# Constant-table products on TensorE in the second mixer phase of a two-block model

## The reference, cut to what matters

```
# mLSTM, per head h and direction, s = source token, t = target token
dw  = exp(dlog - mt)                       # weights by the gates
s   = (q @ k.T) * dw
num = s @ v ;  den = sum(s)
h   = num / max(|den|, exp(-mt))
# differential attention, per head
a   = softmax(q1 @ k1.T / 8) - lam * softmax(q2 @ k2.T / 8)
y   = rmsnorm(a @ v) * g
```

## Time and profile before

| | us |
|---|---|
| median of 3 runs | 4387.51 |
| lowest and highest | 4380.73 to 4388.9 |
| the profiled execution, its own time | 4394.96 |
| span of its trace, first to last instruction | 4392.9 |
| granted TensorE clock, mean over the span | 0.948 of full speed |
| second mixer phase of layer 0 in that trace | 164.9 |
| second mixer phase of layer 1 in that trace | about 100 |

### The profile page before, as it was taken

The page is one execution under the profiler, slowest core; times in us unless marked ns, Lnnn a source line. Parts: engine busy times, 40 slices in busy tenths (PEclk is TensorE's granted clock), DMA queues, the critical chain, the costliest instruction groups (busy, mean ns, idle before and its releaser), DMA issues. The chain is left out here.

```text
span 4392.9 us, 71554 instructions
## 1 busy us (share of the span) xinstructions
PE 4038.2 (92%) x25458; PEld 3554.2 (81%) x25458; DVE 2368.0 (54%) x4150; ACT 1653.4 (38%) x2543; POOL 1542.2 (35%) x605
## 2 busy tenths in 40 slices
PE   7997798978878999999989999999878799999998
PEld 7974388967656999988879999888766699998887
DVE  4012423134552946687548566785555385667855
ACT  3532203232323443333545433334433254333344
POOL 5740006424003986500018866000051188660000
PEclk9997899989779999999999999999988899999999
DMA  5565544522003554444645544445421255444454
GB/s 186 173 216 190 193 134 148 168 84 72 24 5 103 166 163 140 137 144 144 193 146 164 169 138 141 141 146 182 154 88 41 68 164 169 143 138 140 143 182 153
DMA packets 168398, 614.27 MB, mean 140 GB/s; under 512 B 18592, under 2 KB 20000, under 8 KB 167968
## 3 DMA queue, kind: packets, MB, share of 16 engines
q1 hardware_dynamic: 168224, 611.88, 44.7%
HBM read 610.76 MB, written 1.05 MB: 139 GB/s over the span
## 5 line engine op out<-in xcount | busy, mean ns | idle before, releaser
L1729 POOL TENSOR_TENSOR ring_r<-ring,ring_hi 128x1024 fp32r<-128x1024 f32 x408 | 1070.3, 2630 | 1195.2 <-ACT ring_hi L1866 1194.2
L1866 ACT ACTIVATE ring_hi<-ring 128x1024 fp32r<-128x1024 f32 x792 | 837.9, 1059 | 808.7 <-DMA ring<-in_peer_v 485.6
L1744 PE MATMUL bank<-H_r,ring_hi 128*128 128x256 f32 x3264 | 938.6, 288 | 65.4 <-POOL ring_r L1729 64.3
L1745 PE MATMUL bank<-H_r,ring_hi 128*128 128x256 f32 x3264 | 926.0, 284 | 0.0
L1746 PE MATMUL bank<-H_r,ring_r 128*128 128x256 f32 x3264 | 925.4, 284 | 0.0
L280 POOL TENSOR_TENSOR ring_r<-ring,ring_hi 128x1024 fp32r<-128x1024 f32 x183 | 465.2, 2545 | 642.2 <-ACT ring_hi L274 642.2
L1744 PEld LDWEIGHTS bank<-H_r,ring_hi 128*128 128x128 f32 x3264 | 628.0, 192 | 73.4 <-POOL ring_r L1729 45.3
L1745 PEld LDWEIGHTS bank<-H_r,ring_hi 128*128 128x128 f32 x3264 | 628.4, 193 | 0.0
L1746 PEld LDWEIGHTS bank<-H_r,ring_r 128*128 128x128 f32 x3264 | 628.0, 192 | 0.0
L1796 PE MATMUL bank<-ring_hi,H_r 128*128 128x512 f32 x1536 | 483.6, 396 | 5.2 <-DVE ring_r L2040 5.0
L1798 PE MATMUL bank<-ring_r,H_r 128*128 128x512 f32 x1536 | 475.2, 391 | 0.0
(11 more groups left out here) (309 smaller groups left out, 5562.6 us busy)
## 6 DMA issues: line engine op xcount, KB each, us to landing
ring<-in_peer_u SPq DMA_DIRECT2D x384, 512.0 KB, 3.6
ring<-in_peer_v SPq DMA_DIRECT2D x384, 512.0 KB, 3.6
ring<-in_w_in SPq DMA_DIRECT2D x135, 512.0 KB, 3.7
ring<-in_ada SPq DMA_DIRECT2D x96, 512.0 KB, 5.0
ring<-in_w_f SPq DMA_DIRECT2D x72, 512.0 KB, 4.2
ring<-in_w_br SPq DMA_DIRECT2D x24, 512.0 KB, 3.6
ring<-in_w_q SPq DMA_DIRECT2D x24, 512.0 KB, 3.6
ring<-in_w_out SPq DMA_DIRECT2D x16, 512.0 KB, 3.6
```

The source lines that it names most:

```text
L1729: pool.tensor_tensor(ring_lo[:, slot, :], ring[:, slot, :], ring_hi[:, m % NH, :].bitcast(F32), ALU.subtract).then_inc(p_lo, 1)
L1744: pe.matmul(o, hi[:, k], x_hi_[:, kt, :], start=(kt == 0), stop=False)
L1745: pe.matmul(o, hi[:, k], x_lo_[:, kt, :], start=False, stop=False)
L1866: act.activation(ring_hi[:, m % NH, :], ring[:, (n0 + m) % NS, :], ACT.Copy).then_inc(a_hi, 1)
```

## The change

A helper `fill(o)` issues two fp32 products of the identity matrix with the constant table `iota` (128 by 128) into a place `o` of PSUM. Nobody reads what they write: the real product that follows starts its bank afresh (`start=True`). Both operands lie in SBUF in the tile `CS` from the start of the kernel. The calls are:

```
 def products(h, st):
     if h or st >= 2:
         pe.wait_ge(v_w, 8 * h + 2 * st - 2)
+    fill(bank[1 + st % 2][:, t0:t0 + P])
     pe.matmul(bank[1 + st % 2][:, t0:], mk..., mq...)
...
+def fill(o):
+    for _ in range(2):
+        pe.matmul(o, ident, cc("iota"), start=True, stop=True)
...
 def turn_weights(n):
-    pe.wait_ge(v_p, n + 1)
     if n:
         pe.wait_ge(a_pt, n)
+    for k in range(2):
+        fill(bank[6][:, k * P:(k + 1) * P])
+    pe.wait_ge(v_p, n + 1)
...
 def attend(n):
     h = items[n][0]
-    pe.wait_ge(a_pt, n + 1)
     if n:
         pe.wait_ge(v_o, n)
...
+    fill(bank[7][:, 0:P])
+    pe.wait_ge(a_pt, n + 1)
```

## The result

| | before | after |
|---|---|---|
| median of the runs on one chip, us | 4388.9 (5 runs, 4380.73 to 4400.31) | 4419.93 (5 runs, 4417.44 to 4426.26) |
| the profiled execution, us | 4394.96 | 4423.56 |
| span of its trace, us | 4392.9 | 4421.5 |
| phase of layer 0, us at mean granted clock | 163.3 at 0.71 | 182.1 at 0.83 |
| phase of layer 1, us at mean granted clock | 100.2 at 0.74 | 117.9 at 0.78 |

The ratio of the times is 1.0071, with a 95% interval from 1.0052 to 1.009: 31 us slower, 23 to 40. The forecast was 4415, 27 us slower.

What follows compares the result with a forecast made beforehand. TensorE, busy 92% of the span, stood partly at half clock in the two phases, behind idle waits. Fills on the path 45.1 us less 17.8 from the clock: +27.3, 4415 on the median; range 4392 to 4434 for 8 in 10.

Steps and rivals of the forecast that it cites:

- The places of the fills: Both phases: of 104 fills, 34 hide in waits and 70 lie on the path, 42 in layer 0, 28 in layer 1.
- full clock's price: Both phases: 70 fills on the path at 0.45 us each, 31.5 us; by the clock seen at each place, 45 us.
- the two ends at which the prediction called itself wrong: Mean clock of the phases rising from 0.71 and 0.75 to above 0.9, or staying at 0.71 and 0.75.
- (a): Layer 0, quarter 0 of head 1: fills close the gaps between matmuls, clock 0.69 to 1.00, 3.2 us back.
- (b): Layer 0, quarter 0 of head 0, all at half rate: clock rises before its end, 1.7 us back.
- (c): Layer 0, quarter 3 of heads 1 to 3 and the last head's end: a third of 11.3 us back, 3.8.
- (d): Layer 0, quarter 2: denser matmuls bring the clock back earlier, 0.7 us a head, 2.8 us in all.
- (e): Layer 1, quarters 2 and 3: a third of the 19 us that full clock throughout would give, 6.3 us back.
- Rival 1: Both phases: fills cost and the clock gives nothing back, +45 us, 4433; chance 0.18.
- Rival 2: Both phases: clock holds at 2.4 GHz through the idle stretches, 31.5 us cost, 45.5 back, -14 us, 4373.5; chance 0.08.
- Rival 3: Both phases: about half comes back and the path is shorter than counted, +5 us, 4392.5; chance 0.14.
- A page against the row: Layer 0: clock 0.59 in the quarter after 3.39 us idle, 1.00 after 5.78 us without idle; waits throttle the engine.

Runs made afterwards that it cites:

- gap products: Kernel before, without the change's fills, plus single table products ahead of the long waits before `products` of quarter 2 and `values`: 4348.11 us, ratio 0.9922.
- the waits alone: Kernel before with only the order of the two waits in `turn_weights` and `attend` changed, no fills: 4392.81 us, ratio 1.0013.
- fills as well: The changed kernel with all its fills, plus the gap products ahead of the two long waits: 4390.57 us, ratio 1.0001 to the kernel before.
- half the dose: The gap products kernel with half of its products before each wait (8 instead of 16): 4372.46 us, ratio 0.9960 to the kernel before.
- too many gap products: The gap products kernel with 24 instead of 16 before `products` of quarter 2 (layer 1: 16 instead of 10), heads 1 to 3: 4365.26 us, ratio 0.9950.

## Why the prediction was right, and where it was not

**The places of the fills: right.** The three fills of quarter 1 in layer 0 hide, those in quarters 0 and 3 add themselves, and the fill of `products` stands behind its wait and leaves the longest stretches open (12.2 us before, 15.7 after). That was the core of the forecast, and the gap products, the same table product on the other side of the same wait, show it by reversing the sign. That moving the waits alone costs nothing was taken for granted and holds. One place was wrong: the last `attend` of layer 1 was booked as hidden, and its fill stands behind the wait for ACT's root.

**The price of a fill: wrong for `products`.** The step was "A fill is two of them: 0.45 us at full, 0.85 at half", read from the earlier trace rows, where a 128-row product follows a 128-row product. `products` uses 64 rows (the earlier trace rows says `64*128`), and a fill ahead of it measured 0.74 us. In quarter 2, up to DVE's maxima, it measured 0.64. By these two, 16 fills at 0.74 and 16 at 0.64, an estimate, the fills of `products` cost 7.7 us more than booked, of the 10.8 between the measured 42.3 and the booked 31.5. The rest is a balance: the copy and the overrun above (0.9 us in each of two heads), four fills in head 0's quarter 0, which cost 4.3 us at 0.56, and the end of layer 1, 3.4 us longer, where the last `attend` ran at half rate; against them two quarters 3 that ran at 0.77 without the fills and at 1.00 with them.

**What the clock gives back: the sum about right, its terms not.** At full clock's price the forecast said 31.5 less 4.2 makes 27.3. Measured, 42.3 less 5.8 makes 36.5. The clock rose to 0.83 and 0.78, between the two ends at which the prediction called itself wrong. The two layers came out less well than their sum: 18.8 us for 16 and 17.7 for 12. Term by term, with the fills at their booked prices and one trace on each side:

- (a) Quarter 0 of head 1 came back to 10.77 us at 1.00, as forecast. It can't be put down to the fills alone: it did so without them as well. In layer 0, quarter 0 of heads 1 to 3 ran at 1.00 in 15 of 15 in the kernels with fills in it, and in 15 of 21 in those without. That leaves an effect of the fills open. By this the term is worth about 1 us a head, not 3.2 in one.
- (b) Quarter 0 of head 0 went from 8.57 us at 0.50 to 11.66 at 0.56: some 0.3 us back of the four fills' 3.4 at half rate, not 1.7. The other six kernels without fills took 7.4 to 8.6 us there, and against most of them nothing came back.
- (c) Quarter 3 gave little in heads 1 and 2: 0.53 became 0.58, 0.62 became 0.61, and the quarters grew by 1.36 and 2.37 us. The wait before `values` had not been closed. Behind `values(3, 0)` it gave more than its 3.8: from there to the end of the phase it took 12.78 us at 0.73 before and 10.86 at 1.00 after, with four fills more, one of them hidden, the others booked at 2.6 us. Part of that can be chance, since the waits alone had 11.22.
- (d) Quarter 2 of layer 0 did better than forecast in heads 0 to 2 (0.60 to 0.81, 0.64 to 0.76, 0.59 to 0.76) and no better in head 3 (0.58 to 0.60).
- (e) Layer 1, quarters 2 and 3, gave nothing in head 2, the one of the earlier trace rows: 0.59 before, 0.58 after, 3.5 us longer. In heads 0 and 1 they grew by 2.1 us each (0.68 to 0.73, 0.59 to 0.65), and from `products(3, 2)` to the end by 1.1 (0.62 to 0.73). Against four fills at half rate a head, 3.4 us, and five at the end, that is some 5.7 us back, an estimate, near the 6.3 booked, though spread otherwise.

The rest of the rise lies in quarter 1, 0.77 to 0.96 in head 1. There ACT sets the length, so a higher clock is worth little: the quarter grew by 1.1 us, about one fill of `products` at a low clock. A mean clock over a phase is no account of time.

**Hidden fills.** "In layer 1 it is 0.35 us too long [...] so I book 0": at full clock that is right (quarter 1 of head 1 took 8.05 us with gap products and 8.58 with fills as well, which is less than its fill of `products`), at 0.69 the quarter grew by 3.2 us. A cover read at full clock is too small where the clock can be half.

**The rivals.** Rival 1, a clock that gives nothing back, would have cost 45 us at booked prices and more at the true ones; the phases grew by 36.5, at 0.83 and 0.78. Rival 2 is refuted for this change: with the stretches left open the clock did not hold. That the open stretches are the place where the clock is to be had is what the gap products confirm. Its whole return was put at 45.5 us, and the gap products returned 39.5. With fills as well it would have come out 14 us faster by its price of 31.5; at the true 42.3 it comes out at the time of the kernel before. Rival 3 is refuted too: the interval of the change, 23 to 40 us, begins well above its 5.

The prediction says of *A page against the row* that after 5.78 us without idle time the clock was 1.00. It was 1.00 in them; in the quarter behind them, again without idle time, it was 0.69. So idle time ahead is not all that lowers the clock, and what else does stays open.

So the range held the time although the fills of `products` were booked some 8 us too cheap: the phases grew by 36.5 us where 27.3 were forecast, and the medians differ by 31. That the medians came within 5 us of the forecast is partly luck. The scatter of the start-up, 8 us between the two profiled executions, is large enough for the difference between 36.5 and 31; that it is the cause is not shown.

## What to carry to other kernels

Products that only keep TensorE busy must stand ahead of the wait, in a place of PSUM that nobody waits for; behind the wait they are paid in full, and the stretch stays open. Count the stretch and the products in microseconds at full clock, fill most of it and leave a little: half the dose gave half the gain, though it was enough for quarter 2, and half as many again before `products` lost about half of it. When other work is put ahead of such products, count again, since they then reach past the end of the wait. And price an added matmul by the rows of the array that it and its neighbour use, not by its columns alone.

## What the runs showed of the hardware

- A matmul on 64 rows behind one on all 128 starts 0.64 us after a fill's start, behind one on the same 64 rows 0.44 us: the weight load is exposed in the first case and runs beside the fill in the second. That made 0.74 or 0.45 us of one fill in quarter 0. The load is exposed in the other direction too: the fill's own, behind a product on 64 rows, starts with its first matmul (both at 1207.76 after the change).
- With too many gap products TensorE was busy for more of layer 0's phase (149.57 of 155.39 us against 128.29 of 140.71; the half rate itself makes a part of that), yet the mean granted clock was lower (0.81 against 0.93). More busy time does not by itself mean more clock; why it fell there stays open.
- The clock held (0.96 to 1.00) behind waits with up to 2.6 us left idle in layer 0, half the dose, and fell to 0.63 in layer 1 of the same trace behind a wait of at most 0.4 us. The idle piece just ahead did not decide it.
- Executions of programs that are the same up to a landmark reached it up to 17 us apart, and the same quarter of the same work took 7.95 or 11.13 us by the clock it met. Lengths of phases, and counts over several heads and kernels, carried the argument here; single quarters didn't.
